# A decoder step on one core: the moving operand of the linear products is read alternately from two halves of the tokens

## What is computed

```python
def _swiglu(h, w_in, w_out):
    gu = h @ w_in
    gate, up = gu[..., :D_FF], gu[..., D_FF:]
    return (jax.nn.silu(gate) * up) @ w_out
...
    for i in range(DEPTH):
        x = x + 0.5 * _swiglu(_rms_norm(x, w['ffn1_norm'][i]), w['ffn1_w_in'][i], w['ffn1_w_out'][i])
        h = _rms_norm(x, w['mix_norm'][i])
...
        x = x + y
        x = x + 0.5 * _swiglu(_rms_norm(x, w['ffn2_norm'][i]), w['ffn2_w_in'][i], w['ffn2_w_out'][i])
        x = x + (p[i] @ w['ple_w_in'][i]) * jax.nn.sigmoid(
            _rms_norm(x, w['ple_norm'][i]) @ w['ple_w_gate'][i])
```

## Time and profile before

| what | value |
|---|---|
| median of 3 runs | 2749.09 us (2748.33 to 2750.84) |
| the profiled execution, device time | 2749.38 us |
| its span, first to last instruction | 2747.6 us |
| TensorE busy | 2702.4 us (98%) |
| VectorE busy | 1327.1 us (48%) |
| ScalarE busy | 921.6 us (34%) |
| mean granted TensorE clock | 0.992 of full speed |

### The profile page before, as it was taken

One profiled execution on the slowest core, in us unless ns is written; L12 is line 12 of the kernel. 1 busy time (PEld: TensorE's weight loads), 2 busy tenths in 40 slices (PEclk: granted clock), 3 DMA queues, 4 the chain that ended last, 5 costly groups with the idle time before them and its releaser, 6 DMA issues.

```text
span 2747.6 us, 52338 instructions
## 1 busy us (share of the span) xinstructions
PE 2702.4 (98%) x22041; PEld 2609.8 (95%) x22041; DVE 1327.1 (48%) x1715; ACT 921.6 (34%) x1384; POOL 292.2 (11%) x348
## 2 busy tenths in 40 slices
PE   8999999999999999999999999999999999999999
PEld 8999999998887999999999999999986699999999
DVE  4434347765555643333564343434547754343354
ACT  4222124454323332222342222212348732122243
POOL 2000002211224100000110000000133210000011
PEclk9999999999999999999999999999999999999999
DMA  5223222221012232323222332322303422232321
GB/s 141 77 80 88 77 80 88 87 82 30 20 34 76 83 92 77 92 77 89 84 78 85 121 113 77 92 77 84 105 18 108 142 74 84 82 86 78 87 92 54
DMA packets 308138, 225.96 MB, mean 82 GB/s; under 512 B 8270, under 2 KB 301567, under 8 KB 307967
## 3 DMA queue, kind: packets, MB, share of 16 engines
q1 hardware_dynamic: 307280, 224.26, 27.1%
q0 software_dynamic: 576, 0.00, 0.0%
q10 hardware_dynamic: 162, 0.04, 0.0%
HBM read 212.14 MB, written 12.13 MB: 82 GB/s over the span
## 4 chain that ended last, share of the span: by engine, by line
PE 95%; DVE 3%; issue 1%; ACT 1%; POOL 1%; DVEq 0%; POOLq 0%; ACTq 0%
PE ps L537 80%; PE ps L2445 1%; PE ps L556 1%; PE ps L2411 1%; PE ps L1810 1%; PE ps L2453 1%; PE ps L2350 1%; PE ps L1814 1%; PE ps L1558 0%; PE ps L2595 0%; PE ps L2447 0%; PE ps L2448 0%; DVE w_lo L489 0%; PE ps L1660 0%; PE ps L1833 0%
## 5 line engine op out<-in xcount | busy, mean ns | idle before, releaser
L537 PE MATMUL ps<-hx_hi,w_lo 128*128 128x320 f32 (+1 forms) x3730 | 1096.5, 294 | 0.0
L537 PE MATMUL ps<-hx_lo,w_hi 128*128 128x320 f32 (+1 forms) x3730 | 1096.0, 294 | 0.0
L537 PE MATMUL ps<-hx_hi,w_hi 128*128 128x320 f32 (+1 forms) x3730 | 1089.6, 292 | 1.6 <-DVE w_lo L489 1.3
L474 ACT ACTIVATE w_hi<-raw 128x1024 fp32r<-128x1024 f32 (+1 forms) x362 | 375.4, 1037 | 1216.9 <-PE ps L537 1216.2
L537 PEld LDWEIGHTS ps<-hx_hi,w_hi 128*128 128x128 f32 x3730 | 700.2, 188 | 4.7 <-DVE w_lo L489 2.5
L537 PEld LDWEIGHTS ps<-hx_hi,w_lo 128*128 128x128 f32 x3730 | 700.2, 188 | 0.0
L537 PEld LDWEIGHTS ps<-hx_lo,w_hi 128*128 128x128 f32 x3730 | 699.0, 187 | 0.3
L537 PE MATMUL ps<-hid_hi,w_hi 128*128 128x320 f32 (+1 forms) x1920 | 566.5, 295 | 2.2 <-DVE hid_lo L2239 0.5
L537 PE MATMUL ps<-hid_lo,w_hi 128*128 128x320 f32 (+1 forms) x1920 | 567.6, 296 | 0.0
L537 PE MATMUL ps<-hid_hi,w_lo 128*128 128x320 f32 (+1 forms) x1920 | 561.3, 292 | 0.0
L489 DVE TENSOR_TENSOR w_lo<-raw,w_hi 128x1024 fp32r<-128x1024 f32 (+1 forms) x362 | 460.9, 1273 | 108.7 <-ACT w_hi L474 108.6
(11 more groups left out here) (500 smaller groups left out, 2316.7 us busy)
## 6 DMA issues: line engine op xcount, KB each, us to landing
raw<-in_ffn_w_in SPq DMA_DIRECT2D x176, 512.0 KB, 5.0
raw<-in_ffn_w_out SPq DMA_DIRECT2D x64, 512.0 KB, 4.1
raw<-in_a_w_in SPq DMA_DIRECT2D x33, 512.0 KB, 4.6
raw<-in_ffn_w_out SPq DMA_DIRECT2D x32, 384.0 KB, 3.5
raw<-in_ple_w_gate SPq DMA_DIRECT2D x8, 1024.0 KB, 5.2
raw<-in_w_kv SPq DMA_DIRECT2D x16, 512.0 KB, 4.1
k_page<-in_cache_k SPq DMA_DIRECT2D x16, 512.0 KB, 3.6
v_page<-in_cache_v SPq DMA_DIRECT2D x14, 512.0 KB, 4.7
```

What stands on the lines that cost most here:

```text
L474: nc.scalar.activation(w_hi[:, m, 0:k], s.view(m, slot), ACT.Copy).then_inc(w_hi_done, 1)
L537: last = nc.tensor.matmul(TILE[m][:, c0:c1], w[:, m, k], h[:, k, c0:c1], start=k == 0 and a == 0, stop=k == k_all - 1 and a == 2)
```

## The change

The moving operand is no longer a contiguous run of tokens. `woven` views a block of 576 words as 288 pairs: token 0 and token 288, token 1 and token 289, and so on. `columns` takes pairs `c0 // 2` to `c1 // 2` of it. So column 2n of a tile in PSUM holds token n, and column 2n + 1 holds token n + 288. Two words that follow each other in the stream of TensorE lie 1152 bytes apart or 1148 bytes back; each half by itself is read in order. The number of matmuls, their columns, the stationary operand and the writes to PSUM stay.

All that reads a tile out of PSUM has to put the tokens back: `TOKENS[m]` (and `unwoven(PIN)`) is the tile seen as two halves, each of them every second word. `halves` views the SBUF side as two contiguous halves. In the qkv products a first instruction for the 512 prompt tokens becomes two (tokens 0 to 287, and 288 to 511), since they now lie in both halves.

`tail_products` is removed.

```diff
+        def woven(ap):
+            return ap.rearrange("p (c n) -> p n c", c=2)
+        def unwoven(ap):
+            return ap.rearrange("p (n c) -> p c n", c=2)
+        def columns(h, k, c0, c1):
+            return woven(h[:, k])[:, c0 // 2:c1 // 2]
         TILE = tuple(flat[:, 1024 * m + 512 - C0:1024 * m + 512 - C0 + T] for m in range(2))
+        TOKENS = tuple(unwoven(tile) for tile in TILE)
...
-                        last = nc.tensor.matmul(TILE[m][:, c0:c1], w[:, m, k], h[:, k, c0:c1],
+                        last = nc.tensor.matmul(TILE[m][:, c0:c1], w[:, m, k], columns(h, k, c0, c1),
...
-                        last = nc.tensor.matmul(PIN[:, c0:c1], w[:, m, k], h[:, k, c0:c1],
+                        last = nc.tensor.matmul(PIN[:, c0:c1], w[:, m, k], columns(h, k, c0, c1),
...
-            tail_products(pe)
-
-        def tail_products(pe):
...
-                        nc.vector.tensor_tensor(gate_s[:], TILE[0], rs[:], ALU.mult).then_inc(evac[0], 1)
+                        nc.vector.tensor_tensor(halves(gate_s[:]), TOKENS[0], halves(rs[:]), ALU.mult).then_inc(evac[0], 1)
...
-                            nc.vector.scalar_tensor_tensor(x, TILE[m], s.coef, x, ALU.mult, ALU.add).then_inc(evac[m], 1)
+                            nc.vector.scalar_tensor_tensor(halves(x), TOKENS[m], s.coef, halves(x), ALU.mult, ALU.add).then_inc(evac[m], 1)
...
-                            t = TILE[m]
-                            nc.vector.tensor_tensor(xpad[:, m, CP:CP + TP], t[:, 0:TP], rs[:, 0:TP], ALU.mult)
-                            nc.vector.tensor_tensor(seqs(xpad[:, m, CP + TP:], CP + TD)[:, :, CP:], seqs(t[:, TP:T]),
+                            t, left = TOKENS[m], TP - HC
+                            nc.vector.tensor_tensor(xpad[:, m, CP:CP + HC], t[:, 0], rs[:, 0:HC], ALU.mult)
+                            nc.vector.tensor_tensor(xpad[:, m, CP + HC:CP + TP], t[:, 1, 0:left], rs[:, HC:TP], ALU.mult)
+                            nc.vector.tensor_tensor(seqs(xpad[:, m, CP + TP:], CP + TD)[:, :, CP:], seqs(t[:, 1, left:]),
                                                     seqs(rs[:, TP:T]), ALU.mult).then_inc(evac[m], 1)
```

More of the change, by code:

```diff
@@ L894, in ab_dve @@
             dve.wait_ge(new_done, 2 * CT)
-            nc.vector.tensor_tensor(ab[AB_ROWS], TILE[0][AB_ROWS], rs[AB_ROWS], ALU.mult).then_inc(evac[0], 1)
+            nc.vector.tensor_tensor(halves(ab[AB_ROWS]), TOKENS[0][AB_ROWS], halves(rs[AB_ROWS]), ALU.mult).then_inc(evac[0], 1)
             split_lo(dve, split, 0)
@@ L902, in ab_dve @@
             dve.wait_ge(silu_done, s.n["gs"])
-            nc.vector.tensor_tensor(up_s[:], TILE[1], rs[:], ALU.mult).then_inc(evac[1], 1)
+            nc.vector.tensor_tensor(halves(up_s[:]), TOKENS[1], halves(rs[:]), ALU.mult).then_inc(evac[1], 1)
             split_lo(dve, split, 1)
@@ L912, in gate_dve @@
             dve.wait_ge(silu_done, s.n["gs"] + 2 * u + m - 1)
-            nc.vector.tensor_tensor((gate_s, up_s)[m][:], TILE[m], rs[:], ALU.mult).then_inc(evac[m], 1)
+            nc.vector.tensor_tensor(halves((gate_s, up_s)[m][:]), TOKENS[m], halves(rs[:]), ALU.mult).then_inc(evac[m], 1)
             split_lo(dve, split, m)
@@ L3126, in body @@
                             dve.wait_ge(rs_done, s.n["stat"] + s.stats)
-                            nc.vector.scalar_tensor_tensor(s.dst[u * 2 + m], TILE[m], s.scale, rs[:], ALU.mult, ALU.mult
+                            nc.vector.scalar_tensor_tensor(halves(s.dst[u * 2 + m]), TOKENS[m], s.scale, halves(rs[:]), ALU.mult, ALU.mult
                                                            ).then_inc(evac[m], 1)
@@ L3143, in body @@
                             dve.wait_ge(silu_done, u * 2 + (s.n["gs"] + m - 1))
-                            nc.vector.tensor_tensor(buf[:], TILE[m], rs[:], ALU.mult).then_inc(evac[m], 1)
+                            nc.vector.tensor_tensor(halves(buf[:]), TOKENS[m], halves(rs[:]), ALU.mult).then_inc(evac[m], 1)
                             split_lo(dve, split, m)
@@ L3147, in body @@
                             dve.wait_ge(pin_done, u * 2 + (KD * s.n["ple"] + m + 1))
-                            nc.vector.tensor_tensor(prod[:], PIN, buf[:], ALU.mult).then_inc(ple_mul, 1)
+                            nc.vector.tensor_tensor(halves(prod[:]), unwoven(PIN), halves(buf[:]), ALU.mult).then_inc(ple_mul, 1)
                             dve.wait_ge(ple_mul, u * 2 + (KD * s.n["ple"] + m + 1))
```

## The result

The changed kernel takes 2630.37 us in the median of four runs (2629.19 to 2635.27), the kernel before 2749.12 (2748.33 to 2750.84) beside it. The ratio is 0.9571, with an interval of 0.9554 to 0.9587: 118.7 us faster, where 4603 us were forecast. The direction and the size are those of rival A. The woven order is no burden for TensorE; it takes away most of what the contiguous order cost. One further execution of the kernel before, beside the first experiment, took 5814.6 us at the full granted clock; why isn't known, and it is in no comparison.

What follows compares the result with a forecast made beforehand. TensorE, busy 98%, was taken to bound the kernel by number of matmuls times their distance. Span 2747.6 + 1856 for woven matmuls + 0 for readings - 1.9 for the tail, plus 1.8 around it, gave 4603 us; range 2612 to 4780.

Steps and rivals of the forecast that it cites:

- rival A: TensorE's products: words taken from two places come cheaper and the time falls, floor 2613 us, middle 2680; chance 0.18.
- the half pace: Woven matmuls on TensorE: one of two fetched words used, 239.4 ns in place of 131.1, +1856 us; chance 0.42.
- a lost neighbour: Woven operand on TensorE: a fetch brings two neighbouring words but only one is used, 0.831 ns a word.
- the floor of a rival: Lowest time if a woven fetch costs as little as one repeated word, -134 us in the products: 2613 us.
- The Trainium skill's rule: Woven operand in SBUF: one hit on a 16-byte line where two are needed, so the change costs; no price given.
- rival B: TensorE's products: the order of the words doesn't matter, 2747 to 2757 us; chance 0.10.
- L2709 as evidence: Tail matmuls at the half clock, 266 ns for 320 columns, taken as the pace of woven matmuls.
- L2719 as a floor: Tail matmuls on one repeated word, 138 ns for 320 columns: no fetch can be cheaper, gain at most 134 us.
- the count of 17142 matmuls: TensorE's products: 3 x (3730 + 1920 + 64) matmuls at 0.1311 us, 2248 us of the span.
- the tail: 60 matmuls at the kernel's end, with stores beside them: removing them gives -1.9 us, not -11.
- readings with a step of two: VectorE reading tiles from PSUM: 0 to 230 us of its time, hidden by TensorE; taken as 0.
- VectorE hidden in the qkv products: With slower readings and one more instruction a tile, VectorE would be busy 20.9 of 25 us, still behind TensorE.

Runs made afterwards that it cites:

- the first experiment: The kernel before with only the 60 matmuls at its end taken out: 2749.62 us against 2755.88, ratio 0.9985 (0.9974 to 0.9996).
- the groups: Sets of 12 equal matmuls, results unread, put behind the changed kernel's end, each with another operand order; at 320 columns 146.7 ns contiguous, 135.8 woven.

## Why the prediction was wrong, and where it was right

**The step that failed** is "I take the half pace", with its reason that "it would be odd if the same port could give one word a cycle from two places as well". It priced a woven matmul of 320 columns at 266 ns and one of 288 at 239; in the groups they cost 135.8 and 122.5, and the kernel became faster by 118.7 us where it was to become slower by 1854. The mechanism that the prediction feared exists, and is even somewhat dearer than it said: every second word ran at 0.258 us a matmul and 4905.6 us. But which words count as neighbours was assumed from the order of the stream as a whole. The runs show blocks of four words and two alternating sequences; the contiguous order uses two words of a block in each, the woven order four. The price of a lost neighbour is steep from two to one (146.7 to 283) and small from four to two (135.8 to 146.7). The time does lie within 2612 to 4780, but only because that range was drawn down to the floor of a rival; it says nothing for the forecast.

**The Trainium skill's rule**, Advanced Engine Details and Errata, section Memory Cachelines (lines of 16 bytes, two hits on a line to hide the latency), was applied to the whole stream and so spoke against the change. Counted for even and odd places apart, the trace agrees in the main: one word of a line costs 283 ns, two 146.7. It doesn't agree to the letter. The same section of the Trainium skill has a penalty where each access goes to a different cacheline, and the woven stream does just that at 135.8 ns; and two hits aren't quite enough, as three and four are cheaper by 11 ns. The Trainium skill's Vector Engine (DVE) Microarchitecture Reference, section Measured stream behaviour on trn2, has a stream of VectorE between two regions at the full rate, and was placed with rival B; for TensorE the groups at all tested distances from 4 to 2304 words agree.

**L2709 as evidence** The earlier trace rows told nothing on this: it shows that a contiguous stream keeps up at the half clock, not what a stream without neighbours costs at the full one. The group with a step of 14 words happened to run at the lower clock (0.52 in its stretch) and took 295 ns a matmul, where steps of 2 to 9 words took 271 to 300 at 1.00: a hint that the price of a block is a time and doesn't double with the half clock. One group is no proof. **L2719 as a floor** was wrong by a little: one repeated word costs 139 ns at the median again in these runs, the woven stream 135.8. Why the repeated word is dearer stays open.

**Rival A** had the direction and nearly the size, at a chance of 0.18; its floor of 2613 us lies 17 below the result. Its cause ("neighbours getting in each other's way, two places in turn could avoid it") is only half right: each word twice has neighbours one behind the other and costs 136, the order 0, 2, 1, 3 costs 146.7. What counts is how many words of a block each of the two sequences uses. It gave 256 columns 8.7 x 256 / 320 = 7.0 ns and they gained 5.0, since the weight load ends at 111.7; 320 columns gained 9.9 in place of 8.7; and it counted no new waits, where w_lo took 6.5 us more. That the products gain 127 us and not 134 is the first two, the rest are the waits, the 2.9 us of the other matmuls, and 0.6 that the tail gave less. With equal parts, which avoid the floor, the kernel reached 2609.38, below what was called the floor.

**Right were** the count of 17142 matmuls and that a change of their distance passes to the total; that the tail is worth some 2 us and not 11 (1.3 in the trace, 1 to 7 by the runs without it); readings with a step of two at nothing (757 ns against 757); the additional start of an instruction at 0.15 us (839 - 692 = 147 ns), hidden; and VectorE hidden in the qkv products, at 19.52 and 18.75 of 25 us in the changed kernel. Windows there, columns as above:

```profile
450.00:475.00 25.00, 25.00 (x204) 25.00 (x203) 19.52 (x32) 10.00 (x17) 2.37 (x13) 1.00 0.32 100
475.00:500.00 25.00, 25.00 (x205) 25.00 (x204) 18.75 (x31) 11.28 (x20) 2.50 (x14) 1.00 0.32 107
```

**Open**: that there are two readers in the hardware, each with blocks of four words, is inferred from the orders and from the halves of float32; nothing shows them directly. Why four and six places cost 170 and 187 ns and runs of two words 215 is unknown, and so is why every twelfth word costs 400. Weaving the PSUM side, which would show whether writes play a part, wasn't tried.

## What to carry to other kernels

A loss of a few per cent against one column a cycle in long rows of fp32r matmuls is worth a look: take the moving operand from two halves in turn, at least four words apart, and put the columns back where PSUM is read. Here that cost VectorE nothing but one more instruction for each tile of the qkv products. Don't take every second word, which nearly halved the pace here, and don't weave float32, which cost a quarter. Then set the parts anew, so that none lies below the load of its weights (some 264 columns for 128 columns of weights here). And where a price hangs on what counts as neighbours, measure two or three orders by themselves before anything is inferred from a row at another clock.

## What the runs showed that was not expected

- fp32r, 320 columns, granted clock 1.00: 135.8 ns for two places in turn at all tested distances from 4 to 2304 words, 146.7 contiguous, 207 to 215 for runs of two words, 271 to 300 for steps of 2, 3, 4, 5, 8 and 9 words but 400 for every twelfth word.
- Woven matmuls cost columns / 2.4 + 2.5 ns: 122.5 at 288, 135.8 at 320, 162.5 at 384, 215.8 at 512; below some 264 columns they cost the load of the weights, 111.7 ns for 128 columns of them, 85.0 for 96 and 58.3 for 64.
- A contiguous operand that starts one word later costs 150.8 ns, two words later 147.2, four words later 145.3.
- float32, per record of 320 columns: 269 ns contiguous and in runs of four words, 280 for every second word, 563 for every fourth, 339 woven.
